# Gates ahead of values in the projection order, a new start and DVE order of the mLSTM chunks, and an output projection begun inside the attention

## The chip, the cores and the metric

The kernel runs on one core of one Trainium2 chip. The metric is the device time of one execution in microseconds. Engines: TensorE (PE, matmuls), ScalarE (ACT), VectorE (DVE), GpSimd (POOL) and SyncE (SP, which issues most DMAs). They run beside each other and meet at semaphores.

## The reference

Two transformer blocks over 1024 tokens of width 1024. The change touches only the mixer of the first:

```python
proj = h @ w_in          # query/key of the mLSTM, v_ml, o_ml, gates, q_at, kv_at
qk_ml = silu(causal_dwconv(qk_ml))
# per chunk and head, with the running state C, n:
sqk = (q @ k.T) * exp(dmat - m_t)
h   = (sqk @ v + w_inter * (q @ C.T)) / max(|den|, exp(-m_t))
h_ml = rms_norm(h, ml_norm_g) * sigmoid(o_ml)
o_at = sliding_window_attention(rope(q_at), rope(k_at), v_at, sinks)
o_at = rms_norm(o_at, attn_norm_g)
y = concatenate([h_ml, o_at]) @ w_out
x = x + g1 * rms_norm(y, post_mix_g)     # g1 and the like: silu(c) @ w_ada
```

A feed-forward block and a whole second block follow; they take the other 1988 us and are not touched.

## The kernel before

Each fp32 product is three fp32r matmuls of 128x128 by 128x512: operands and weights are split into a high and a low part (hhi, hlo; whi, wlo). A weight tile (128 columns, all eight rows of tiles, 512 KB) is loaded by SP, its high part is cut by ACT (`split_hi`, L214) and its low part by DVE (`split_lo`, L219), and it costs PE 48 matmuls, 10.9 us in full (`product`, L294 to L296).

**Product stage.** The input projection has N_IN = 22 tiles: 0 to 5 query, key and value of the attention, 6 to 13 mLSTM query and key with a convolution of three DVE steps (L1154), 14 to 17 mLSTM values, 18 to 21 output gates (sigmoid, spilled to DRAM by POOL). PE's product t waits for `up_free`, that is for the evacuation of product t-2. Beside this DVE adds up the last four adaLN segments, 32 rows of w_ada of 512 KB, each loaded by SP into one of three slots (L960) and added by DVE (L400, L401) at three per tile from tile 8 on (`late_at`). After the product behind the one in which a segment closes, PE waits for its eight rows and reduces it. In DVE's program the rows of tile t stand behind its convolution. The masks are added (L940) and exponentials taken (L946) in tiles 20 and 21.

**Chunks.** Eight chunks of 128 tokens. PE per chunk c: `outputs(c)` (L1396, L1399), `turn_back(c-2)` (L1408), `turn(c+2)` (L1369 to L1371), `update(c+1)` (L1381). ACT copies tokens (L1332, L1333), squares (L1339) and takes the root (L1346, L1348), and in chunks 2 to 5 copies attention keys (L1558). DVE per chunk: copy of the last head (L1442), new state (L1453), denominators (L1463 to L1469), gating of c-2 (L1486), scaling of c-1 (L1476 to L1480), weights of c+2 (L1438). `outputs(c+1)` waits for `scale(c-1)`, whose PSUM bank it writes. Two slots hold the gate tiles that SP loads back (L1280), each behind `c_done`; the gain rows (L1253) stand behind it in the same queue. The first query block of the attention is loaded (L1690) after all of them.

**Attention.** Eight blocks of 128 queries, two units each: scores (PE), maxima (DVE, L1897), exponentials (ACT, L1710), scaling (POOL, L1778), transposes (PE, L1828), split of the probabilities (ACT L1731, DVE L1924), values (PE, L1850 to L1852). Blocks 1 to 6 run in a hardware loop of three trips. Its operands lie in hhi and hlo.

**Output projection.** In the next block (a barrier lies between), `Mix` makes the eight operand tiles: 0 to 3 the mLSTM's, 4 to 7 the attention's after its norm. PE multiplies weight tiles 0 and 1 by operand tiles 0 and 1, then does eight fp32 sum matmuls of 128x512 over the squares (`sum_squares`, L338), then the other operand tiles (L363 to L365); the third product follows.

## Time and profile before

| | |
|---|---|
| median of 3 runs | 2482.6 us (2482.34 to 2487.81) |
| profiled execution, its own time | 2482.53 us |
| its span, first to last instruction | 2480.7 us |
| mean granted TensorE clock | 0.991 |
| PE, DVE, ACT, POOL busy | 96%, 50%, 34%, 14% |

Timelines give each instruction (or run of equal ones, xN) its start and duration. In brackets stands how long the engine was idle before it and what it waited for. Matmuls are pipelined, so their durations overlap and the distance of two starts is what one costs. 0.0 is the first instruction.

### The profile page before, as it was taken

Reading aid. Unit: us, or ns where it says so; the run is one execution under the profiler, and the core shown is the slowest. Engines: PE = TensorE matmul, PEld = TensorE weight load, DVE = VectorE, ACT = ScalarE, POOL = GpSimd, SP = SyncE. Lnnn points to the kernel's source line nnn. Section 1 sums busy time; section 2 is a strip of 40 time slices with the busy share of each in tenths; the row PEclk is TensorE's granted clock in tenths of the full one; section 3 lists DMA queues with packets and bytes.
Section 4 is the critical chain, followed back from the end, with each engine's and each line's share of the span. In section 5 each row is a group of like instructions: output and inputs, shape, how many; then the busy total and the mean of one; then the engine's idle time right before and its main releaser. Section 6 shows DMA issues by size and latency. Waiting matters only on the chain. (4 is left out here: it accounts for less than half of the span.)

```text
span 2480.7 us, 28558 instructions
## 1 busy us (share of the span) xinstructions
PE 2387.0 (96%) x10880; PEld 1927.7 (78%) x10880; DVE 1247.8 (50%) x1492; ACT 833.0 (34%) x1234; POOL 346.5 (14%) x268
## 2 busy tenths in 40 slices
PE   7999978899999999999998989999999999999999
PEld 5788877576888888888876767767888888888887
DVE  6467357437544444444456489963533333333334
ACT  5232267634322222222244368862311111111111
POOL 1120044132000000000032456621000000000000
PEclk9999999999999999999999999999999999999999
DMA  8246532122211111111124220012111111111111
GB/s 325 76 137 210 166 99 74 60 74 89 67 51 43 41 51 51 44 49 51 43 102 141 77 68 26 17 52 68 52 51 51 51 51 41 43 51 51 51 47 72
DMA packets 192733, 183.78 MB, mean 74 GB/s; under 512 B 8505, under 2 KB 170633, under 8 KB 192145
## 3 DMA queue, kind: packets, MB, share of 16 engines
q1 hardware_dynamic: 189984, 175.21, 22.1%
q0 software_dynamic: 2208, 7.37, 0.9%
q8 instruction: 49, 0.80, 0.1%
q14 instruction: 27, 0.22, 0.0%
q10 hardware_dynamic: 465, 0.17, 0.0%
HBM read 154.38 MB, written 28.34 MB: 74 GB/s over the span
## 5 line engine op out<-in xcount | busy, mean ns | idle before, releaser
L294 PE MATMUL ps<-hhi,whi 128*128 128x512 f32 x1696 | 662.8, 391 | 4.5 <-DVE wlo L219 2.0
L296 PE MATMUL ps<-hhi,wlo 128*128 128x512 f32 x1696 | 660.0, 389 | 0.0
L295 PE MATMUL ps<-hlo,whi 128*128 128x512 f32 x1696 | 659.8, 389 | 0.0
L219 DVE TENSOR_TENSOR wlo<-raw,whi 128x1024 fp32r<-128x1024 f32 x178 | 226.4, 1274 | 379.5 <-ACT whi L214 379.4
L294 PEld LDWEIGHTS ps<-hhi,whi 128*128 128x128 f32 x1696 | 318.3, 188 | 72.7 <-DVE wlo L219 2.4
L295 PEld LDWEIGHTS ps<-hlo,whi 128*128 128x128 f32 x1696 | 318.4, 188 | 67.1 <-issue 1.2
L296 PEld LDWEIGHTS ps<-hhi,wlo 128*128 128x128 f32 x1696 | 318.3, 188 | 66.4
L214 ACT ACTIVATE whi<-raw 128x1024 fp32r<-128x1024 f32 x178 | 184.5, 1049 | 387.4 <-PE ps L2420 286.4
L2573 DVE TENSOR_TENSOR arena<-arena,ps 128x1024 f32<-128x1024 f32 x152 | 185.4, 1220 | 128.2 <-PE ps L2420 127.3
L2418 PE MATMUL ps<-hid_hi,whi 128*128 128x512 f32 x608 | 237.6, 391 | 0.0
L2419 PE MATMUL ps<-hid_lo,whi 128*128 128x512 f32 x608 | 236.7, 389 | 0.0
L2420 PE MATMUL ps<-hid_hi,wlo 128*128 128x512 f32 x608 | 236.6, 389 | 0.0
L758 POOL TENSOR_TENSOR cbuf<-cbuf 128x512 f32<-128x512 f32 (+1 forms) x54 | 80.0, 1489 | 890.6 <-ACT cbuf L745 887.6
L2537 DVE SCALAR_TENSOR_TENSOR cbuf<-ps,par,cbuf 128x1023 f32<-128x1023 f32 x44 | 56.4, 1282 | 226.0 <-ACT cbuf L2444 226.0
L1778 POOL TENSOR_TENSOR cbuf<-cbuf,attn_stats 128x1024 f32<-128x1024 f32 x80 | 151.5, 1894 | 95.4 <-DVE attn_stats L1917 95.4
L2418 PEld LDWEIGHTS ps<-hid_hi,whi 128*128 128x128 f32 x608 | 114.1, 188 | 26.8 <-DVE arena L2573 3.3
L2420 PEld LDWEIGHTS ps<-hid_hi,wlo 128*128 128x128 f32 x608 | 114.1, 188 | 23.9
L2419 PEld LDWEIGHTS ps<-hid_lo,whi 128*128 128x128 f32 x608 | 114.1, 188 | 23.5
L2444 ACT ACTIVATE cbuf<-ps,par 128x1024 f32<-128x1024 f32 x44 | 53.0, 1205 | 222.7 <-PE ps L296 220.4
L2550 DVE TENSOR_TENSOR cbuf<-ps,cbuf 128x1024 f32<-128x1024 f32 x22 | 26.9, 1225 | 175.1 <-PE ps L296 156.5
L2458 ACT ACTIVATE hid_hi<-cbuf 128x1024 fp32r<-128x1024 f32 x44 | 46.5, 1057 | 203.1 <-DVEq L2552 110.0
L1828 PE MATMUL ps<-identF,cbuf 128*128 128x128 f32 x640 | 93.0, 287 | 17.2 <-POOL cbuf L1778 14.3
(343 smaller groups left out, 3363.8 us busy)
## 6 DMA issues: line engine op xcount, KB each, us to landing
raw<-in_w_up SPq DMA_DIRECT2D x66, 512.0 KB, 3.6
raw<-in_w_down SPq DMA_DIRECT2D x44, 512.0 KB, 3.4
raw<-in_w_in SPq DMA_DIRECT2D x32, 512.0 KB, 5.1
arena<-in_w_ada SPq DMA_DIRECT2D x32, 512.0 KB, 5.1
raw<-in_w_gate SPq DMA_DIRECT2D x22, 512.0 KB, 3.6
raw<-in_w_out SPq DMA_DIRECT2D x16, 512.0 KB, 3.7
arena<-x_park SPq DMA_DIRECT2D x2, 4096.0 KB, 12.2
x_park<-arena SPq DMA_DIRECT2D x4, 2048.0 KB, 8.8
```

The costliest lines, as they stand in the source:

```text
L214: nc.scalar.activation(whi[:, w.off % RING, :], raw[:, w.off % RAW, :], ACT.Copy).then_inc(hi_done, 1)
L219: nc.vector.tensor_tensor(wlo[:, w.off % RING, :], raw[:, w.off % RAW, :], whi[:, w.off % RING, :].bitcast(F32), ALU.subtract).then_inc(lo ...
L294: nc.tensor.matmul(acc[:, tok], whi[:, s, ws], hhi[:, k, tok], start=(k == 0), stop=False)
L295: nc.tensor.matmul(acc[:, tok], whi[:, s, ws], hlo[:, k, tok], start=False, stop=False)
L296: mm = nc.tensor.matmul(acc[:, tok], wlo[:, s, ws], hhi[:, k, tok], start=False, stop=(k == DK - 1))
L758: nc.gpsimd.tensor_tensor(total, total, cbuf[:, self.slot(r, k), tok], ALU.add).then_inc(self.added[r], 1)
L1778: nc.gpsimd.tensor_tensor(p, p, st[:, sl, 16:16 + q].unsqueeze(2).to_broadcast([P, q, T // q]), ALU.mult).then_inc(S["scaled"], 1)
L1828: mm = nc.tensor.transpose(ps_t[:, (4 * h + k) * P:(4 * h + k + 1) * P], src, identF[:, :])
L2418: nc.tensor.matmul(o, whi[:, s, ws], hidhi[:, p, tok], start=(r == 0), stop=False)
L2419: nc.tensor.matmul(o, whi[:, s, ws], hidlo[:, p, tok], start=False, stop=False)
L2420: mm = nc.tensor.matmul(o, wlo[:, s, ws], hidhi[:, p, tok], start=False, stop=(r == 1))
L2573: nc.vector.tensor_tensor(y[:, fo, :], y[:, fo, :], down[fo % 2][:, :], ALU.add)\
```

## The change

Gates become tiles 14 to 17 and values 18 to 21. The adaLN rows go four to a tile. Masks and exponentials move to tiles 18 to 20, the broadcast rows are loaded earlier, and PE's first turn waits head by head for the last value tiles. Gate tiles get a third slot, the first query block is loaded ahead of the chunk loop, ACT copies the keys in chunks 0 to 3 and DVE subtracts them in chunks 3 and 5; DVE scales c-1 right behind the new state. In the attention the operands move so that hhi 0 to 2 and hlo 0 are free: POOL makes high parts of tiles 0 to 2 in block 0, and squares and adds of the first 512 tokens in blocks 5 to 7; DVE makes the low parts. In the last unit PE does the first half's sum and operand tiles 0 and 1. The attention's loop has two trips and blocks 5 and 6 are unrolled. Behind the barrier the norm goes by halves, with squares added in pairs by POOL before two sum matmuls per half. Left out below: index changes to the third slot, to the tile numbers of gates and values, and the removed body of `Mix`.

```diff
...
                 r = o - T_IN
-                return columns(a["w_in"], w + (20 if r < 2 else 14 if r < 6 else -6), 8 if r < 6 else 0)
+                shift = 20 if r < 2 else 14 if r < 6 else -6 if r < 14 else -2 if r < 18 else -10
+                return columns(a["w_in"], w + shift, 8 if r < 6 else 0)
...
         def kind_of(t):
-            return "qkv" if t < 6 else "conv" if t < 14 else "v" if t < 18 else "o"
+            return "qkv" if t < 6 else "conv" if t < 14 else "o" if t < 18 else "v"
...
-            return range(max(0, 3 * (t - LATE_FROM)), max(0, min(late_rows, 3 * (t - LATE_FROM + 1))))
+            return range(max(0, 4 * (t - LATE_FROM)), max(0, min(late_rows, 4 * (t - LATE_FROM + 1))))
...
+        EXP_FROM = 18
...
                       .then_inc(late_loaded[n % 3], 16)
-                if t == N_IN + 2:
+                if t == N_IN - 1:
...
                     nc.scalar.activation(query_hi_of[n % 2], cbuf[:, (t - 2) % 4, :], ACT.Copy).then_inc(query_hi, 1)
-                if t >= N_IN - 2:
-                    act.wait_ge(g_dve, 13)
-                    for c in range(4 * (t - N_IN + 2), 4 * (t - N_IN + 3)):
+                if t in (EXP_FROM + 1, EXP_FROM + 2):
+                    if t == EXP_FROM + 1:
+                        nc.scalar.preload_act_table_set(LN_EXP)
+                        act.wait_ge(g_dve, 13)
+                    for c in range(4 * (t - EXP_FROM - 1), 4 * (t - EXP_FROM)):
...
                     modulate(ADA_FIRST + seg, down[1][:, seg * DK:(seg + 1) * DK]).then_inc(late_done, 1)
-                if t == N_IN - 2:
-                    for c in range(NB):
+                if t in (EXP_FROM, EXP_FROM + 1):
+                    for c in range(4 * (t - EXP_FROM), 4 * (t - EXP_FROM + 1)):
...
-        def chunk_sp(sp):
+        def chunk_sp(sp, first_query):
...
                 sp.wait_ge(spilled[i], 64)
-            sp.wait_ge(used, N_IN)
-            for b in range(2):
+            multiplied(sp, At(N_IN - 1))
+            for b in range(3):
                 sp.dma_start(gate_tok[b], spill[:, 0:4, tok(b)]).then_inc(gate_in[b], 16)
+            for i in range(2):
+                sp.wait_ge(hi_stored[i], 64)
+            first_query()
...
                     gain_load(sp, c + 2)
-                sp.wait_ge(c_done, c - 1)
-                sp.dma_start(gate_tok[c % 2], spill[:, 0:4, tok(c)]).then_inc(gate_in[c % 2], 16)
-            for i in range(2):
-                sp.wait_ge(hi_stored[i], 64)
+                if c >= 3:
+                    sp.wait_ge(c_done, c - 2)
+                    sp.dma_start(gate_tok[c % 3], spill[:, 0:4, tok(c)]).then_inc(gate_in[c % 3], 16)
...
                 rstd(c)
-                if 2 <= c < 6:
-                    keys.act_key(act, (c - 2) // 2, c % 2)
+                if c < 4:
+                    keys.act_key(act, c // 2, c % 2)
...
                 for h in range(ML_H):
+                    if c == 0:
+                        pe.wait_ge(up_free, N_IN - 1 + h)
...
                     new_state(c)
-                denominators(c)
+                    if c:
+                        scale(c - 1)
+                    denominators(c)
+                else:
+                    denominators(c)
+                    scale(c - 1)
...
                     gated(c - 2)
-                if c:
-                    scale(c - 1)
...
                     weigh(c + 2)
-                else:
-                    keys.dve_keys(dve, c + 2 - NB)
+                if c in (3, 5):
+                    keys.dve_keys(dve, (c - 3) // 2)
...
             kn = T + pad
-            o = 4 * kn
-            khh = lflat[:, 0:2 * kn].rearrange("p (g t) -> p g t", g=2)
-            klo = lflat[:, 2 * kn:o].rearrange("p (g t) -> p g t", g=2)
+            k0 = 0 if full else T
+            o = k0 + 4 * kn
+            khh = lflat[:, k0:k0 + 2 * kn].rearrange("p (g t) -> p g t", g=2)
+            klo = lflat[:, k0 + 2 * kn:o].rearrange("p (g t) -> p g t", g=2)
...
             else:
-                pths, ptls = [[hflat[:, 1024 * (2 * i + j):1024 * (2 * i + j + 1)].rearrange("p (k x) -> p k x", x=ptile)
+                pths, ptls = [[hhi[:, 3 + 2 * i + j, :].rearrange("p (k x) -> p k x", x=ptile)
                                for i in range(2)] for j in range(2)]
-                vband = [hflat[:, 4096 + 512 * i:4096 + 512 * (i + 1)] for i in range(2)]
+                vband = [hhi[:, 7, half(i)] for i in range(2)]
...
                 body(At(0), True)
-                with eng.Fori(0, 3) as i:
+                with eng.Fori(0, 3 if full else 2) as i:
...
                     body(At(2, i, 2), True)
+                if not full:
+                    body(At(5), True)
+                    body(At(6), True)
...
+            def mixing(n, at):
+                return not full and n.i is None and n.off == at
...
                             fetch(n + 1)
-                    lead.sp(sp)
-                    query_blocks(sp, lambda: fetch(At(0)), body)
+                    if full:
+                        lead.sp(sp)
+                        query_blocks(sp, lambda: fetch(first_block), body)
+                    else:
+                        lead.sp(sp, lambda: fetch(first_block))
+                        query_blocks(sp, lambda: None, body)
...
                             u, gr = unit(n, e), group(n, e)
+                            if mixing(n, 7) and e == 1:
+                                mix.act_first_root(act)
...
                             band(At(0))
+                            mix.pool_high(pool, 0)
...
                                 lead.pool_unit(pool, e)
+                            if mixing(n, 0):
+                                mix.pool_high(pool, 1 + e)
+                            if mixing(n, 5) and e == 0:
+                                pool.wait_ge(S["out"], NB)
+                            if mixing(n, 5) or mixing(n, 6):
+                                mix.pool_square(pool, 2 * (n.off - 5) + e)
+                            if mixing(n, 6) and e == 0:
+                                mix.pool_add(pool, 0)
+                            if mixing(n, 7) and e == 0:
+                                mix.pool_add(pool, 1)
...
                                 scores(n, e + 2)
+                            if mixing(n, 7) and e == 1:
+                                pe.wait_ge(S["sink_arg"], 2 * NB)
+                                mix.pe_first_sum(pe)
+                                pe.wait_ge(S["exp"], 2 * NB)
+                                mix.pe_tile(pe, 0)
...
                                     values(gr_before(n, e), ((e - 1) // units) % 2, unit(n, e) + (-1))
+                        if not more and not full:
+                            mix.pe_tile(pe, 1)
...
                             split_probs(n, e)
+                            if mixing(n, 0) and e == 1:
+                                mix.low(dve, 0)
+                            if mixing(n, 7) and e == 0:
+                                mix.low(dve, 1)
+                                mix.low(dve, 2)
...
             def __init__(self):
...
+                self.squared, self.added, self.summed, self.log_done, self.rstd_done = (
+                    sem("mix_" + x) for x in ("squares", "squares_added", "sums", "logs", "rstd"))
...
+                self.op_hi, self.op_lo, self.lows = sem("mix_hi"), sem("mix_lo"), DK + 4
+                self.u0 = n_up[0]
...
+            def square_of(self, h, j):
+                return cbuf[:, (2 if h == 0 else 0) + j // 2, half(j % 2)]
+            def sums(self, h):
+                return down[1][:, half(1)] if h == 0 else down[0][:, half(0)]
+            def root(self, h):
+                return self.square_of(h, 1)
+            def pool_high(self, pool, j):
+                nc.gpsimd.tensor_copy(hhi[:, j, :], self.tile(j)).then_inc(self.op_hi, 1)
+            def pool_square(self, pool, j):
+                q = qa[:, j, half(0)]
+                nc.gpsimd.tensor_tensor(self.square_of(0, j), q, q, ALU.mult).then_inc(self.squared, 1)
+            def pool_add(self, pool, pair, h=0):
+                total = self.square_of(h, 2 * pair)
+                pool.wait_ge(self.squared, 4 * h + 2 * pair + 2)
+                nc.gpsimd.tensor_tensor(total, total, self.square_of(h, 2 * pair + 1), ALU.add).then_inc(self.added, 1)
+            def pool(self, pool):
+                for pair in range(2):
+                    self.pool_add(pool, pair, 1)
+            def pe_sum(self, pe, h):
+                for pair in range(2):
+                    pe.wait_ge(self.added, 2 * h + pair + 1)
+                    mm = nc.tensor.matmul(self.sums(h), onesF[:, :], self.square_of(h, 2 * pair), start=(pair == 0),
+                                          stop=(pair == 1))
+                mm.then_inc(self.summed, 1)
+            def pe_first_sum(self, pe):
+                self.pe_sum(pe, 0)
+            def pe_tile(self, pe, k, halves=(0, 1)):
+                if k == 0:
+                    for t in range(2):
+                        pe.wait_ge(up_free, self.u0 + t + 1)
+                        pe.wait_ge(lo_done, T_OUT + t + 1 + RAW)
+                for t in range(2):
+                    s = (T_OUT + t) % RING
+                    ws = slice(k * P, (k + 1) * P)
+                    for h in halves:
+                        pe.wait_ge(self.op_lo, k + 1 if k < 4 else 4 * h + k + 1)
+                        tok, o = half(h), up[t][:, half(h)]
+                        nc.tensor.matmul(o, whi[:, s, ws], hhi[:, k, tok], start=(k == 0), stop=False)
+                        nc.tensor.matmul(o, whi[:, s, ws], hlo[:, k, tok], start=False, stop=False)
+                        mm = nc.tensor.matmul(o, wlo[:, s, ws], hhi[:, k, tok], start=False, stop=(k == DK - 1))
+                    if k == DK - 1 and halves[-1] == 1:
+                        mm.then_inc(used, 1)
+            def pe_pair(self, pe, w, u0):
+                self.pe_tile(pe, 2)
+                self.pe_tile(pe, 3)
+                self.pe_sum(pe, 1)
+                for h in range(2):
+                    for k in range(4, DK):
+                        self.pe_tile(pe, k, (h,))
+            def act_root(self, act, h):
+                r = self.root(h)
+                act.wait_ge(self.summed, h + 1)
+                nc.scalar.activation(r, self.sums(h), ACT.Ln, bias=eps, scale=1.0 / 512).then_inc(self.log_done, 1)
+                act.wait_ge(self.log_done, h + 1)
+                nc.scalar.activation(r, r, ACT.Exp, scale=-0.5).then_inc(self.rstd_done, 1)
+            def act_first_root(self, act):
+                self.act_root(act, 0)
...
             def act(self, act):
...
+                def hi(h, j):
+                    act.wait_ge(self.product, 4 * h + j - 3)
+                    nc.scalar.activation(hhi[:, j, half(h)], qa[:, j - 4, half(h)], ACT.Copy).then_inc(self.op_hi, 1)
+                nc.scalar.activation(hhi[:, 3, :], self.tile(3), ACT.Copy).then_inc(self.op_hi, 1)
...
+                    nc.scalar.activation(self.square_of(1, j), qa[:, j, half(1)], ACT.Square).then_inc(self.squared, 1)
...
+                    hi(0, j)
+                self.act_root(act, 1)
+                for j in range(4, DK):
+                    hi(1, j)
+                    if j >= 6:
+                        split_hi(act, At(T_OUT + j - 6 + AHEAD))
+            def low(self, dve, j):
+                dve.wait_ge(self.op_hi, j + 1)
+                nc.vector.tensor_tensor(hlo[:, j, :], self.tile(j), hhi[:, j, :].bitcast(F32), ALU.subtract)\
+                  .then_inc(self.op_lo, 1)
...
             def dve(self, dve):
...
+                self.low(dve, 3)
+                for h in range(2):
+                    dve.wait_ge(self.rstd_done, h + 1)
+                    for i in range(5):
+                        if i < 4:
+                            q = qa[:, i, half(h)]
+                            nc.vector.scalar_tensor_tensor(out=q, in0=q, scalar=par_col("attn_norm_g", i),
+                                                           in1=self.root(h), op0=ALU.mult,
+                                                           op1=ALU.mult).then_inc(self.product, 1)
+                        if i >= 1:
+                            j = 3 + i
+                            dve.wait_ge(self.op_hi, 4 * h + j + 1)
+                            nc.vector.tensor_tensor(hlo[:, j, half(h)], qa[:, i - 1, half(h)],
+                                                    hhi[:, j, half(h)].bitcast(F32), ALU.subtract).then_inc(self.op_lo, 1)
...
+        mixing_norm = Mix()
+        attention("attn", False, FirstLead, cbuf[:, 2, :], cbuf[:, 3, :], mixing_norm)
```

## Rows read from the trace of the kernel before

**Rows 1.** Windows: bounds, length; busy PE, PEld, DVE, ACT, POOL; clock, DMA, GB/s.

```profile
318.30:380.60 62.30, 43.73 (x341) 42.03 (x340) 38.08 (x118) 35.58 (x113) 26.84 (x26) 0.92 0.31 90
```

**Rows 2.** Timeline of PE, chunks: start, duration, instruction, count, [idle before, releaser].

```profile
325.98 0.48 PE L1369 MATMUL ps<-identF,arena 128*128 128x128 f32 x1 [5.73 <-ACT chunk_work L1333]
...
330.93 1.06 PE L1396 MATMUL ps<-chunk_work 128*128 128x129 f32 x8
...
341.50 0.46 PE L1396 MATMUL ps<-chunk_work 128*128 128x129 f32 x2 [2.31 <-DVE chunk_work L1480]
...
347.03 0.46 PE L1396 MATMUL ps<-chunk_work 128*128 128x129 f32 x2 [0.41 <-DVE chunk_work L1480]
...
351.10 1.06 PE L1381 MATMUL ps<-chunk_work 128*128 128x129 f32 x8
...
353.56 0.46 PE L1396 MATMUL ps<-chunk_work 128*128 128x129 f32 x2 [1.40 <-DVE chunk_work L1480]
...
371.19 0.46 PE L1396 MATMUL ps<-chunk_work 128*128 128x129 f32 x2 [3.07 <-DVE chunk_work L1480]
...
380.61 0.47 PE L1808 MATMUL ps<-bandR,identR 128*128 128x512 f32 x1 [2.88 <-DMA gateR<-query_parts]
```

**Rows 3.** Timeline of ACT, the beginning of the chunks.

```profile
316.41 4.79 ACT L946 ACTIVATE arena<-arena,gateF 128x128 f32<-128x128 f32 x16
...
323.55 1.28 ACT L1350 ACT_TABLE_LOAD   x1
...
324.84 0.60 ACT L1332 ACTIVATE chunk_work<-ps 128x512 f32<-128x512 f32 x1
```

**Rows 4.** Timeline of DVE, chunk 3.

```profile
349.30 1.12 DVE L1453 SCALAR_TENSOR_TENSOR chunk_work<-chunk_work,gateF,ps 128x129 f32<-128x129 f32 x4
...
353.13 0.28 DVE L1480 TENSOR_SCALAR chunk_work<-chunk_work 128x128 f32<-128x128 f32 x1
```

**Rows 5.** Timeline of PE, end of the attention and first pair of w_out.

```profile
450.79 1.09 PE L1828 MATMUL ps<-identF,cbuf 128*128 128x128 f32 x8 [1.18 <-POOL cbuf L1778]
...
455.33 0.40 PE L1852 MATMUL ps<-hhi 128*64 128x512 f32 x1
...
460.61 0.77 PE L363 MATMUL ps<-hhi,whi 128*128 128x512 f32 x1 [4.88 <-DVE hlo L2057]
...
467.63 7.03 PE L338 MATMUL ps<-cbuf,onesF 128*128 128x512 f32 x16
...
492.48 0.50 PE L294 MATMUL ps<-hhi,whi 128*128 128x512 f32 x1 [0.67 <-ACT arena L2122]
```

**Rows 6.** Timeline of ACT in the same stretch.

```profile
458.14 2.00 ACT L2026 ACTIVATE hhi<-arena 128x1024 fp32r<-128x1024 f32 x2 [1.61 <-PEq L1677]
...
490.49 1.03 ACT L745 ACTIVATE cbuf<-ps 128x1024 f32<-128x1024 f32 x1 [5.29 <-PE ps L365]
```

**Rows 7.** Timelines of DVE, ACT and SP in the product stage.

```profile
185.64 4.05 DVE L401 SCALAR_TENSOR_TENSOR arena<-arena,small 128x1024 f32<-128x1024 f32 x3
...
191.45 1.21 ACT L1052 ACTIVATE cbuf<-ps,par 128x1024 f32<-128x1024 f32 x1 [3.68 <-PE ps L296]
...
232.31 2.38 SPq L960 DMA_DIRECT2D arena<-in_w_ada  x3
...
235.94 1.28 DVE L401 SCALAR_TENSOR_TENSOR arena<-arena,small 128x1024 f32<-128x1024 f32 x1 [0.46 <-DMA arena<-in_w_ada]
```

**Rows 8.** Timelines of POOL and DVE; last, the page's group of weight splits.

```profile
343.68 1.27 POOL L1289 TENSOR_TENSOR lead_work<-arena 128x512 f32<-128x512 f32 x1 [3.12 <-PE ps L1399]
...
440.64 1.90 POOL L1778 TENSOR_TENSOR cbuf<-cbuf,attn_stats 128x1024 f32<-128x1024 f32 x1 [2.11 <-DVE attn_stats L1917]
...
549.28 12.48 POOL L758 TENSOR_TENSOR cbuf<-cbuf 128x512 f32<-128x512 f32 x8
...
553.29 2.32 DVE L219 TENSOR_TENSOR wlo<-raw,whi 128x1024 fp32r<-128x1024 f32 x1
...
L219 DVE TENSOR_TENSOR wlo<-raw,whi 128x1024 fp32r<-128x1024 f32 x178 | 226.4, 1274 | 379.5 <-ACT whi L214 379.4
```

79 lines of the change are left out of this document (19 added, 60 removed).

## The prediction, made before the changed kernel was run

> **What bounds it now.** I read the page first: TensorE is busy for 96% of the span, so time can be won only where it stands idle or does work that can go. The slices of the page show that in few places, and windows cut at the stage bounds say where: in the chunks of the mLSTM (318.3 to 380.6) PE is busy 43.7 of 62.3 us at a granted clock of 0.92 [rows 1], while in w_out's first pair it is busy, but in part with fp32 sums and at half clock. The third reading is PE's timeline across these stages, with what released each wait [rows 2], and then the engine that was late: ACT at the start [rows 3], DVE in the chunks [rows 4], and in the tail PE's own extra work, the block's end and ACT [rows 5, 6]. The product stage ahead of 318.3 has no PE wait at all, so there the change can only lose [rows 7].
>
> All sums are on the clock of the profiled execution (2482.53 us around a span of 2480.7). The median of the runs is 2482.6, so a difference carries over unchanged.
>
> **A. Product stage, late adaLN rows by fours: +2.3.** Moving gates to tiles 14 to 17 reorders loads of equal size and costs nothing: an evacuation is one ACT pass either way. But tiles 8 to 15 now bring four w_ada rows each, not three, and segments close at tiles 9, 11, 13 and 15, where PE waits for all eight rows one product later. In tile 9 the convolution's end lets DVE begin adding at 185.64, and three adds last 4.05, or 1.33 apart [rows 7]. Three slots hold three rows, so SP can ask for the block's fourth row only when the first is added, at 186.97. The nearest landing is that of the row asked for at 232.31 and used at 235.94, 3.63 later [rows 7]. So the fourth is there at 190.6 and added at 191.95. PE would want the segment at about 191.2, just ahead of the evacuation at 191.45 [rows 7]: 0.75 late. Three segments close in convolution tiles, 3 x 0.75 = 2.3; the fourth closes in a gate tile without convolution, and I cost it at nothing. Bounds: 0 if a row lands in 2.8, and +9 if each lands 2.3 later, as may be when several loads share the DMA engines. Queued behind DVE's wait are the split of a weight tile, used two products later, and the next convolution, which has over 5 us of slack; SP's next loads wait behind the row too, with a tile or more in hand. The exponents and exponentials (4.79 per four chunks on ACT [rows 3]) move to tiles 18 to 20, where one tile of 10.9 us holds them, an evacuation and a split: nothing.
>
> **B. The beginning of the chunks: -6.8.** Now PE has turned chunk 0 and then waits 5.73 before it turns chunk 1 at 325.98, because ACT first ends the exponentials begun at 316.41 (4.79), loads a table, does the last sigmoid, loads a table at 323.55, and only then copies chunk 0's tokens at 324.84 [rows 2, 3]. After the change ACT has one copy of the last value tile (about 1.0, ending at 319.6); PE turns heads 0 to 2 beside it and head 3 at 319.7 to 320.1, tokens are copied from 320.35 to 321.4, PE goes on at 321.5. The idle time is then 1.3 instead of 5.73, and after 2.31 us idle at 341.5 later in this stage the clock was still full, so chunk 1's turn takes 1.8 and not 3.5. With the update (0.9) the first outputs begin at 324.1, not 330.93 [rows 2]: -6.8. If the clock falls all the same it is -4.5. The Trainium skill (ScalarE: Activation LUTs, What ACT_TABLE_LOAD costs) puts a switch of tables at 2.66, of which 1.38 is a drain. Here the load at 323.55 is followed by its first activation at 324.84, 1.29 later [rows 3]; no row shows a drain. By the page the two loads would be worth 2.8 more, by the rows they are inside the 6.8; the rows decide.
>
> **C. The chunks' order: -7.3.** DVE did denominators, gating of chunk c-2 and only then the scaling of c-1, which frees the PSUM bank that outputs c+1 want. For outputs 4: the new state is under way at 349.30 and lasts 1.12, scaling ends only at 353.4 (353.13 + 0.28), and PE starts at 353.56 [rows 2, 4]. Right behind the new state (0.15 and 0.56 and 0.28 with their hand-overs, some 0.85) scaling ends at 351.2, so outputs 4 could begin at 351.4. PE's own work from outputs 3 at 347.03 to the end of the update that begins at 351.10 takes 4.96 (351.10 + 0.89) [rows 2]. So PE becomes its own bound at 4.96 per chunk, against 6.5 here and 6.0 on average from outputs 3 to 7 ((371.19 - 347.03) / 4). The new queue on DVE is 4.3 us per chunk, on ACT 4.3 with a key copy (1.05, now in chunks 0 to 3). The two key subtractions (1.2) fall behind the last weighing of chunks 3 and 5, where DVE would wait. Outputs 3 to 7: three times 4.96 and a last 4.5 (no turn to fill in) = 19.4 against 24.2, -4.8. Outputs 0 to 3: 13.2 against 16.1, -2.9. I give back 0.4 for small DVE steps that stand behind Pool now and then. The third gate slot takes SP's wait for c_done off the gain rows behind it in the queue; that only keeps them from being late. Bounds -3 to -8.5.
>
> **D. The chunks' end: -3.2.** From outputs 7 (371.19) to the first scores (380.61) go 9.4 [rows 2]. The scores waited 2.88 for the query DMA, asked for only when all chunk loads had gone; it is now ahead of them. What is late next is the scaling of chunk 7: denominators, squares, root and scaling end 6.2 after outputs 7 start, since the key subtraction and the gating ahead are gone. Bounds -2 to -3.7 (with the clock).
>
> **E. In the attention: +1.4.** Pool gains three copies of 128x1024 in block 0, four squares of 128x512 and one add in blocks 5 and 6, one add in block 7. A 128x512 operation took it 1.27, and scaling 1.89 in a pitch of 4.0 to 4.2 [rows 8], so one square fits behind each scaling (3.16), but not square and add (4.43): +0.3 to +0.6 once. In block 0 the second copy ends some 0.9 after the next scaling is wanted and DVE's subtraction (1.2) has 0.9 to 1.1 of idle time to hide in: +0.8. Nothing else is moved past; the two unrolled blocks replace one loop trip. Bounds 0 and +4.
>
> Rows for a rule that speaks against this: DVE's weight split at 553.29 took 2.32, against a mean of 1.27 for all 178, while Pool ran eight adds from 549.28 on [rows 8]. The Trainium skill (SBUF - State Buffer, SBUF: two separate sides) says that a VectorE operation with two SBUF inputs and a GpSimd operation that reads SBUF exclude each other for the whole instruction. The row agrees; the sum above takes the slots as free, and a rival below takes them as not.
>
> **F. Output projection: -10.2.** Now the last product of the values starts at 455.33, ACT begins the next block at 458.14, PE at 460.61 after 4.88 idle, first at half clock; eight fp32 sums take 7.03; the third product starts at 492.48 [rows 5, 6]. After: two sums (2 x 0.81) and 12 products (12 x 0.2275 = 2.73) go ahead of the last transposes, 12 more ahead of the last values. Of these 7.1 us 1.18 fall into idle time ahead of the last transposes (450.79) and the rest of the difference into the wait ahead of the last values: these start their last product 4.6 later, at 459.95, and the next block begins at 462.75 [rows 5]. Left are 6 tiles x 12 x 0.2275 = 16.4 and two sums = 18.0: end at 480.8 against 491.65. ACT and DVE have each operand ahead of PE: first half-tile product at 467, wanted at 470; second half at 473.9, wanted at 475.5. The evacuation begins at 480.3 instead of 490.49, product three at 482.3: -10.2. The x load (4 MB) is asked for 7.6 earlier, product three comes 10.2 earlier; the weight tile behind it is wanted over 10 us later, so no loss. If PE's 2.4 idle at the block's end halves its clock, it is -8.8. Bounds -7.5 and -11.
>
> **Sum.** 2.3 - 6.8 - 7.3 - 3.2 + 1.4 - 10.2 = -23.8; 2482.5 - 23.8 = 2458.7. The 1988 us behind shift as a whole.
>
> **Rivals.** (1) The chunk pitch doesn't fall: the root of c-1 (squares 1.6 and root 0.6 behind the token copies) takes the place of the order. For it: ACT does 4.3 per 4.96; against: it ends some 0.6 ahead of need. Then C loses 5.5: 2464. (2) Rows land late in A: 5.5 instead of 3.6 makes the three stalls 2.6 each: 2464 to 2466. For it: loads bunch. (3) Pool and DVE shut each other out: eleven new Pool operations, each costing 1.05 as at 553.29, are 11.6 in place of 1.4: 2469. Against: most stand where DVE waits for ACT. The rule cited under E is this case's. (4) The change doesn't do what it says in F: PE's idle time there is only moved, since the projection's early part delays the last values and the operands behind them: F is -4, 2465. (5) Slower: the fourth row again. It stalls PE by its landing less 2.9, three times; the change as a whole loses more than 7.4 only if that eats 31 us, from a landing of 13.3 on. The landing shown is 3.63 [rows 7]. 2490.
>
> **Chances.** Forecast 0.62, own range 2453 to 2463; (1) 0.13, (2) 0.09, (3) 0.06, (4) 0.05, (5) 0.02; two or more of them together 0.03, near no change. Range 2452 to 2470. A measurement here can tell 0.3%, 7.4 us, from no change: faster 0.94, within 0.03, slower 0.03.
>
> **What would show it.** A: PE waits for a DVE add of 0.5 to 1 us, three times ahead of the adaLN reductions. B: first outputs 5.8 us behind the last product. C: outputs 4.9 to 5.2 apart. D: no DMA wait ahead of the scores. E: attention pitch still 4.0 to 4.2. F: the third product starts 19.5 us after ACT's first step of that block. It would be wrong if outputs stay 6 apart, if PE waits for an operand in the half tiles, or if the clock falls at the seams.

## The result, and the profile after

The changed kernel takes 2473.1 us (median of 6 runs, 2471.57 to 2476.78), the kernel before 2485.2 beside it (6 runs, 2482.34 to 2487.81): ratio 0.995, 95% interval 0.994 to 0.9961. It is faster, by half of what I forecast: 12.1 us in place of 23.8. The two profiled executions are 2482.53 and 2475.31, only 7.2 apart, since the one sits low among its kernel's runs and the other high; the table is in their clock, and adds up to the 7.4 between their spans. A negative number is time won.

| Stage | before | after | forecast | measured |
|---|---|---|---|---|
| start to the first convolution tap | 143.02 | 142.37 | 0 | -0.65 |
| tap to the end of the last product (A) | 175.30 | 187.98 | +2.3 | +12.68 |
| to outputs 0 (B) | 12.61 | 5.83 | -6.8 | -6.78 |
| outputs 0 to 7 (C) | 40.26 | 35.80 | -7.3 | -4.46 |
| outputs 7 to first scores (D) | 9.42 | 8.34 | -3.2 | -1.08 |
| first scores to third product (E, F) | 111.87 | 101.85 | -8.8 | -10.02 |
| third product to the end | 1988.22 | 1991.13 | 0 | +2.91 |
| span | 2480.7 | 2473.3 | -23.8 | -7.4 |

One stage holds most of the miss. The product stage, where PE had no wait at all before, now loses 12.7 us. The timeline of PE in the changed kernel (start, duration, instruction; in brackets the idle time before it and who ended it) has three waits there, all at the fp32 sums that close an adaLN segment:

```profile
194.55 3.57 PE L345 MATMUL ps<-onesF,arena 128*128 128x1 f32 x16 [3.79 <-DVE arena L402]
...
223.62 1.92 PE L345 MATMUL ps<-onesF,arena 128*128 128x1 f32 x16 [1.07 <-DVE mod L406]
...
248.82 1.92 PE L345 MATMUL ps<-onesF,arena 128*128 128x1 f32 x16 [1.41 <-DVE mod L406]
```

The first is 3.79 us, where I had said 0.75, and the sums behind it take 3.57 in place of 1.84 to 1.92: half clock (the granted clock is 0.50 from 194 to 203, that is 1.2 and not 2.4 GHz). The windows of ten microseconds (busy time of PE, PEld, DVE, ACT, POOL; then the granted clock) show how long it lasts:

```profile
190.00:200.00 10.00, 6.21 (x25) 5.37 (x24) 7.32 (x7) 2.15 (x2) 0.00 (x0) 0.66 0.74 262
200.00:210.00 10.00, 10.00 (x39) 8.05 (x38) 6.58 (x6) 2.12 (x2) 0.00 (x0) 0.83 0.74 258
210.00:220.00 10.00, 10.00 (x46) 8.29 (x45) 6.77 (x6) 2.27 (x2) 0.00 (x0) 1.00 0.09 20
...
250.00:260.00 10.00, 10.00 (x41) 8.20 (x41) 5.65 (x5) 2.75 (x3) 0.58 (x1) 0.83 0.86 292
```

Who was late is in the other timelines. ACT's, in the same stretch:

```profile
181.87 1.06 ACT L214 ACTIVATE whi<-raw 128x1024 fp32r<-128x1024 f32 x1 [6.58 <-DMA raw<-in_w_in]
182.84 1.19 ACT L1056 ACTIVATE cbuf<-ps,par 128x1024 f32<-128x1024 f32 x1
188.06 1.06 ACT L1059 ACTIVATE arena<-cbuf 128x1024 f32<-128x1024 f32 x1 [4.02 <-DVE cbuf L1158]
194.70 1.06 ACT L214 ACTIVATE whi<-raw 128x1024 fp32r<-128x1024 f32 x1 [5.58 <-DMA raw<-in_w_in]
195.66 1.19 ACT L1056 ACTIVATE cbuf<-ps,par 128x1024 f32<-128x1024 f32 x1
```

ACT waits 5 to 7 us for a weight tile, eight times in this stage. The tap (L1056), which begins a tile's convolution and so frees its PSUM, stands behind that split in ACT's order: it starts at 182.84, not when its product ends. SyncE's queue and DVE say why the tile is late:

```profile
176.27 13.29 SPq L962 DMA_DIRECT2D arena<-in_w_ada  x4
189.67 0.38 SPq L208 DMA_DIRECT2D raw<-in_w_in  x1
```

```profile
178.92 1.28 DVE L402 SCALAR_TENSOR_TENSOR arena<-arena,small 128x1024 f32<-128x1024 f32 x1 [1.28 <-DMA arena<-in_w_ada]
182.97 1.23 DVE L219 TENSOR_TENSOR wlo<-raw,whi 128x1024 fp32r<-128x1024 f32 x1 [2.76 <-ACT whi L214]
184.11 3.91 DVE L1158 SCALAR_TENSOR_TENSOR cbuf<-ps,par,cbuf 128x1023 f32<-128x1023 f32 x3
187.94 4.05 DVE L402 SCALAR_TENSOR_TENSOR arena<-arena,small 128x1024 f32<-128x1024 f32 x3
193.21 1.29 DVE L402 SCALAR_TENSOR_TENSOR arena<-arena,small 128x1024 f32<-128x1024 f32 x1 [1.21 <-DMA arena<-in_w_ada]
```

The four row loads from 176.27 on take up 13.29 us of the queue. The last of them is the fourth row of the product: its slot is free when DVE has added the product's first row, at 187.94 + 1.33 = 189.3, and there the queue goes on. It lands in about 3.9 (added at 193.21), near the 3.63 of [rows 7]. But the load of the next weight tile goes out only at 189.67, behind it, and ACT has it at 194.70, where it wanted it at 189.1. In the kernel before the load in the same place goes out 8 us ahead of its split, which waits for nothing; but two tiles later a split does wait, if only 0.24 (SyncE's queue and ACT):

```profile
178.74 1.14 SPq L208 DMA_DIRECT2D raw<-in_w_in  x1
...
186.73 1.04 ACT L214 ACTIVATE whi<-raw 128x1024 fp32r<-128x1024 f32 x1
...
208.83 1.06 ACT L214 ACTIVATE whi<-raw 128x1024 fp32r<-128x1024 f32 x1 [0.24 <-DMA raw<-in_w_in]
```

### The profile page after: what moved, and what is told of

The parts are those of the page before. It is cut to its first block and busy times, and to the rows that moved or that the text cites. A ratio compares the mean times of both kernels' runs of the same rounds, so it can differ in the third digit from the quotient of the medians.

```text
span 2473.3 us, 28496 instructions
## 1 busy us (share of the span) xinstructions
PE 2388.8 (97%) x10872; PEld 1930.1 (78%) x10872; DVE 1252.9 (51%) x1500; ACT 824.5 (33%) x1233; POOL 359.3 (15%) x279
## 5 line engine op out<-in xcount | busy, mean ns | idle before, releaser
L1862 PE MATMUL ps<-identF,cbuf 128*128 128x128 f32 x640 | 92.3, 287 | 17.0 <-POOL cbuf L1802 12.8
```

The lines of the kernel that those rows point to most:

```text
L1862: mm = nc.tensor.transpose(ps_t[:, (4 * h + k) * P:(4 * h + k + 1) * P], src, identF[:, :])
```

## Experiments

Four kernels first, to tell the queue from the landing, and a side question on the chunks. (The fourth of them, with its companion, was made last, after all the others.) Kernels were run in batches, each beside the kernel before; where two batches are compared, the ratio to it says more than the time. In all of them the stage is measured from the first tap to the end of the last product.

**Only the rows by fours, on the kernel before.**

```diff
-            return range(max(0, 3 * (t - LATE_FROM)), max(0, min(late_rows, 3 * (t - LATE_FROM + 1))))
+            return range(max(0, 4 * (t - LATE_FROM)), max(0, min(late_rows, 4 * (t - LATE_FROM + 1))))
```

> The kernel before with one edit of the change: adaLN rows by fours (4 per product from product 8 on, in 3 slots) in place of threes. Theory Q (SyncE's queue): the fourth row of a product waits in SyncE's queue for the add of the first row of the same product, and the load of the next weight tile stands behind it, so ACT gets its weight tile 5 to 7 us late and evacuates late. The last product then ends 10 to 13 us later than the 318.3 of the kernel before, and the time is before +10 to +13. Theory L (the prediction's step A: only the landing of the fourth row counts, 0.75 us at each of three segment ends): before +2.3.

Measured: 2500.9 against 2488.14, ratio 1.0048 (1.0031 to 1.0065), 12.8 us slower. The stage takes 189.17 (+13.9), with PE waits of 3.16, 1.00 and 0.98, as theory Q had it. The loss belongs to this one edit; without the rest the kernel would have become slower than before.

**The changed kernel with rows by threes.**

```diff
-            return range(max(0, 4 * (t - LATE_FROM)), ...
+            return range(max(0, 3 * (t - LATE_FROM)), ...
...
-                if t == N_IN - 1:
+                if t == N_IN:
                     sp.wait_ge(rows_stored, 16)
...
-        EXP_FROM = 18
+        EXP_FROM = 19
...
-                if t in (EXP_FROM, EXP_FROM + 1):
-                    for c in range(4 * (t - EXP_FROM), 4 * (t - EXP_FROM + 1)):
+                if t == EXP_FROM + 1:
+                    for c in range(NB):
                         exponents(dve, c)
```

> The changed kernel with its rows by threes again (products 8 to 18); the exponents and exponentials are one and two products later (20; 20 and 21), and SyncE asks for the exponent rows behind the load of tile 22. All else as in the changed kernel. Theory Q: the last product ends at 317 to 319, not at 330.4, everything behind it keeps its lengths, and the time is that of the changed kernel less 11 to 12.5, some 2461 to 2462. Theory L: less 2.3, 2471. A third theory (the 12 us come from values behind gates, or from the earlier exponentials): no gain at all.

Measured: 2462.13, ratio 0.9898 (0.9881 to 0.9914). The stage is 175.30 again, to the hundredth, without a wait, so the gates ahead of the values cost nothing there. The exponentials are in tiles 20 and 21 again in this kernel, as in the kernel before, so it says nothing on them; the next one, which has them early, does. It pays elsewhere: outputs 0 begin 8.44 behind the last product and not 5.83. PE waits 0.81 in the first turn of the beginning and 1.18 ahead of the second here (the changed kernel has the 1.18 alone), and then runs slow: step B's -4.5 for a clock that falls (12.61 to 8.44 is -4.2).

**A fourth slot.** Rows stay by fours.

```diff
-        late_row = [ar(48 + 4 * i, D) for i in range(3)]
+        late_row = [ar(48 + 4 * i, D) for i in range(3)] + [ar(32, D)]
...
-                    if n >= 3:
-                        sp.wait_ge(late_added, n - 2)
...
+                    if n == 3:
+                        sp.wait_ge(rows_stored, 16)
+                        sp.wait_ge(gains_stored, 16)
+                        sp.wait_ge(g_pe, 1)
+                    if n >= 4:
+                        sp.wait_ge(late_added, n - 3)
...
```

> The changed kernel with rows by fours, and a fourth slot for them (in the space of the values, which is written from product 18 on): the fourth row of a product waits only for the product before. Number, size and order of the loads stay. Theory Q: SyncE is no longer held inside a product, the 5 to 7 us waits of ACT for weight tiles go, the last product ends at 317 to 320, time as with threes to within 1.5 us (2461 to 2463). Theory of the landings (four rows and a weight tile share the DMA engines, so they come late whatever the queue does): last product still at 325 or later, 2468 or more. A PE wait at the ends of the segments of 0 to 1 us each may stay in both.

Measured: 2460.61, ratio 0.9894 (0.9878 to 0.9911). The stage takes 175.52 and PE has no wait in it. The same 32 rows and the same weight tiles move in the same order; only what SyncE waits for and the place of one row in four are different. So it isn't the amount of traffic, and the exponentials in tiles 19 and 20 cost 0.2 at most. ACT still waits for one weight tile, 7.08 ahead of its split at 247.62, and PE doesn't notice it.

**One weight tile later in the queue.** Three slots, rows by fours, one number:

```diff
-                for n in late_at(t - 2):
+                for n in late_at(t - 3):
```

> The changed kernel (three slots, rows by fours) with one number changed: SyncE asks for the rows of a product one weight tile later in its queue (rows of product t-3 behind the load of tile t, not of product t-2). The fourth row still waits for the first add of its product, but the load behind it is one that ACT wants a whole product later. Theory Q: ACT's waits of 5 to 7 us for weight tiles go, and what is left of the 12.7 us that the product stage lost is the fourth row's own landing ahead of the adaLN reductions, the prediction's 2.3 (0 to 3.5): last product's end 177.5 after the first tap (175.3 in the kernel before, 188.0 in the changed kernel), time 2461 to 2464. If the landing of four rows, not the queue, were the cause, the stage stays at 184 or more and the time at 2469 or more.

And beside it the changed kernel unaltered:

> The changed kernel unaltered, on the same chip as the one above. All theories: 2473, ratio to before 0.995; the product stage takes 188 from the first tap to the last product's end and the stage behind the third product 1988 to 1991.6, by the number of norm sums that meet half clock.

Measured: swap 2468.44, ratio 0.993 (0.9916 to 0.9943); the unaltered changed kernel beside it 2472.12, ratio 0.9944 (0.993 to 0.9957). The intervals overlap a little, but the slowest run of swap (2470.6) is faster than the fastest of the other (2471.24). This is between my two expectations, and it splits the loss. The groups of instructions of ACT from 175 to 290 (count, busy time, mean ns, idle time before them) in the changed kernel, and then in this one:

```profile
L214 ACT ACTIVATE whi<-raw 128x1024 fp32r<-128x1024 f32 x10 | 10.6, 1057 | 45.4 <-DMA raw<-in_w_in 45.4
```

```profile
L214 ACT ACTIVATE whi<-raw 128x1024 fp32r<-128x1024 f32 x10 | 10.5, 1047 | 0.0
```

45.4 us of waiting for weight tiles are gone, and yet the stage takes 183.56: 8.3 more than before. What is left is the fourth row's own landing and what follows it, in PE's timeline of this kernel:

```profile
192.99 1.95 PE L345 MATMUL ps<-onesF,arena 128*128 128x1 f32 x16 [0.84 <-DVE arena L402]
194.79 0.48 PE L295 MATMUL ps<-hhi,whi 128*128 128x512 f32 x1
...
219.44 1.92 PE L345 MATMUL ps<-onesF,arena 128*128 128x1 f32 x16 [0.98 <-DVE mod L406]
```

and in its windows:

```profile
190.00:200.00 10.00, 9.16 (x42) 7.38 (x41) 8.62 (x8) 3.21 (x3) 0.00 (x0) 0.83 0.69 243
...
240.00:250.00 10.00, 9.05 (x43) 7.39 (x42) 7.20 (x8) 2.92 (x3) 0.58 (x1) 0.86 0.99 360
```

The waits are 0.84, 0.98 and 0.95: 2.8 in all, and the 2.3 that step A had worked out, nearly. But behind two of the three PE runs eight products at a pitch of 0.43 and not 0.227. For all kernels I add up the waits, and the time lost to slow clock (each product's pitch over 0.3, less 0.227, without the 0.5 that the same count gives at full clock, and what the sums take over 1.9):

| Kernel | stage | waits of PE | slow clock |
|---|---|---|---|
| before, threes | 175.30 | 0 | 0 |
| fourth_slot | 175.52 | 0 | 0 |
| swap | 183.56 | 2.77 | 4.7 |
| changed | 187.98 | 6.27 | 5.7 |
| changed, again | 189.48 | 5.52 | 7.6 |
| keys_late | 189.21 | 5.29 | 7.7 |
| fours_alone | 189.17 | 5.14 | 7.6 |

Waits and clock together are all but 0.7 to 1.1 of each loss, and in four of the five kernels the clock is the larger part. In the last three and in swap 1.6 to 2.9 of it stands at 147 to 156, behind 3 us of small fp32 products of 4x4 and 4x8 and with no wait near; the other kernels, the changed one in its first trace among them, have the same products there and no slow clock. All four have rows by fours in three slots. Whether that plays a part stays open.

**Key subtractions in chunks 6 and 7.**

```diff
-                if c in (3, 5):
-                    keys.dve_keys(dve, (c - 3) // 2)
+                if c in (6, 7):
+                    keys.dve_keys(dve, c - 6)
```

> The changed kernel with DVE's two key subtractions (1.22 us each) in chunks 6 and 7, where they were before, not in 3 and 5. Theory K (the subtraction of chunk 5 makes the scaling late that outputs 7 wait for): the wait of 3.60 us ahead of outputs 7 falls to 2.0 to 2.6, PE's clock stays full there, outputs 3 to 7 take 20.5 and not 21.9, outputs 7 to the first scores 6.2 to 7.2 and not 8.3; in all -2 to -3.5, 2470. Theory P (Pool's operations that run beside DVE's small SBUF operations make the scaling late): the wait stays within 0.5 of 3.6, and the subtraction in chunk 7 is hidden behind the root; within 1 us of the changed kernel.

Measured: 2473.68, ratio 0.9938 (0.9922 to 0.9955), where the changed kernel has 0.995 (0.994 to 0.9961) and, in its second batch, 0.9944: no gain that can be told. The wait ahead of outputs 7 falls from 3.60 to 2.46 and outputs 3 to 7 from 21.94 to 20.08, as theory K said, and the way to the first scores is 8.69 and not 8.34. But the unaltered kernel's second trace has 3.21 and 20.77, and swap, with the subtractions in 3 and 5, has 2.67: one trace can't carry a difference of this size. Whether the place matters isn't shown.

The second four are on the fourth-slot kernel, which no longer has the disturbance of step A.

**Chunks 3 and 6.**

```diff
-                if c in (3, 5):
-                    keys.dve_keys(dve, (c - 3) // 2)
+                if c in (3, 6):
+                    keys.dve_keys(dve, (c - 3) // 3)
```

> The fourth-slot kernel with DVE's two key subtractions in chunks 3 and 6 (not 3 and 5, nor 6 and 7). Theory K: in chunk 6 the subtraction stands behind everything that outputs 7 wait for, and not ahead of the scaling of chunk 7, so outputs 3 to 7 take about 20.1 as in keys_late (against 21.15), and outputs 7 to the first scores 6.2 as in fourth_slot (8.69 in keys_late): 1 us under fourth_slot, ratio to before 0.989. Theory P (Pool's beat sets this stage): no change to 0.5 us.

Measured: 2459.77, ratio 0.9893 (0.9877 to 0.991), the same as fourth_slot's 0.9894 to what can be told. Outputs 0 to 7 take 34.16 and not 35.01, then 8.32 and not 6.20: its outputs 7 ran at half clock. The 0.8 us are less than the 1.2 by which outputs 0 to 7 differ in two traces of the unaltered changed kernel (35.80 and 34.63), so whether the place is worth anything stays open.

**DVE's order in the chunks undone.**

```diff
                 if c + 1 < NB:
                     new_state(c)
-                    if c:
-                        scale(c - 1)
-                    denominators(c)
-                else:
-                    denominators(c)
-                    scale(c - 1)
+                denominators(c)
                 if c >= 2:
                     gated(c - 2)
+                if c:
+                    scale(c - 1)
```

> The fourth-slot kernel with DVE's order in the chunks as before: denominators of c, gating of c-2, then the scaling of c-1; nothing else. If the order is what shortens the chunks (the prediction's step C, 7.3 us, of which 4.8 from outputs 3 to 7): outputs 3 to 7 take 24 to 25 and not 21.15, outputs 0 to 3 16, waits for the scaling of 0.4 to 1.5 us ahead of each outputs again, time 4 to 6 us over fourth_slot, some 2466. If the pitch fell for another reason (exponentials, gates and query out of the way): within 1.5 us of fourth_slot.

Measured: 2467.08, ratio 0.9929 (0.9905 to 0.9952). Outputs 0 to 3 take 17.12 (13.86 in fourth_slot), 3 to 7 25.33 (21.15), and PE waits 1.16 to 2.16 for the scaling ahead of every outputs from 2 to 6. The order is worth 7.4 in the trace and 6.5 in the medians (8.7 by the ratios). It is the whole of step C: with the old order outputs 0 to 7 take 42.45, not even the 40.26 of the kernel before, so the chunks' other edits shorten nothing there by themselves.

**Pool's gating multiplication made short.** The output lacks most of the norm's gains.

```diff
-                nc.gpsimd.tensor_tensor(gate_tok[c % 3], gate_tok[c % 3],
-                                        par_col("ml_norm_g", 0, 4).unsqueeze(2).to_broadcast([P, ML_H, P]),
+                nc.gpsimd.tensor_tensor(gate_tok[c % 3][:, :, 0:4], gate_tok[c % 3][:, :, 0:4],
+                                        par_col("ml_norm_g", 0, 4).unsqueeze(2).to_broadcast([P, ML_H, 4]),
                                         ALU.mult).then_inc(c_gain, 1)
```

> The fourth-slot kernel, but Pool multiplies by the norm's gains only 4 of the 128 positions of each head of a chunk's gates, so eight operations of 1.04 us become short ones; the rest of that multiplication is left out. Theory P (DVE's smallest operations with both operands in SBUF, L1469 to L1486 of the changed kernel, last 0.8 to 1.0 instead of 0.15 to 0.28 where they meet a Pool operation): four to nine such long ones become two to four, outputs 0 to 7 take 1.5 to 2.5 less than 35.0, ratio to before 0.0008 lower. If PE's own work and the root's chain set the pitch: 0.5 us or less, though the DVE operations get shorter all the same.

Measured: outputs 0 to 7 take 32.74 where fourth_slot has 35.01; 2456.31, ratio 0.9878 (0.9862 to 0.9895), some 4 us under fourth_slot's, with intervals that overlap. The timelines of DVE and then of Pool in fourth_slot show the cause, chunk 4:

```profile
347.90 1.00 DVE L1486 TENSOR_TENSOR chunk_work<-chunk_work 128x4 f32<-128x4 f32 x1
348.94 0.56 DVE L1488 TENSOR_TENSOR chunk_work<-ps,chunk_work 128x384 f32<-128x384 f32 x1
349.41 0.28 DVE L1490 TENSOR_SCALAR chunk_work<-chunk_work 128x128 f32<-128x128 f32 x1
349.60 0.15 DVE L1473 TENSOR_TENSOR chunk_work<-ps,gateF 128x3 f32<-128x3 f32 x1
349.67 0.94 DVE L1473 TENSOR_TENSOR chunk_work<-chunk_work,gateF 128x1 f32<-128x1 f32 x1
```

```profile
347.84 1.04 POOL L1311 TENSOR_TENSOR chunk_work<-chunk_work,par 128x512 f32<-128x512 f32 x1
349.46 1.13 POOL L1305 TENSOR_TENSOR chunk_work<-chunk_work,gateF 128x516 f32<-128x516 f32 x1 [0.57 <-ACT chunk_work L1343]
```

and in the kernel with the short multiplication, the same instruction of DVE:

```profile
346.07 0.17 DVE L1486 TENSOR_TENSOR chunk_work<-chunk_work 128x4 f32<-128x4 f32 x1
```

An operation on four columns takes 1.00, and ends at 348.90, when Pool's ends (347.84 + 1.04). The one on three columns that reads PSUM takes 0.15 at 349.60, with Pool at work beside it; the next, on one column with both operands in SBUF, takes 0.94 and ends at 350.61, again with Pool's (350.59). Of 19 such operations between outputs 0 and 7 (one or four columns, both operands in SBUF), seven are long in fourth_slot (5.1 us too much in all), eight in the changed kernel (5.9) and two in the kernel with the short multiplication (1.0). The unaltered changed kernel's second trace has five (3.4), and there outputs 0 to 7 take 34.63 in place of 35.80. The scaling of the fourth head (L1490, 128x128, one tensor from SBUF) is long too at times: 0.78 and 0.99 in place of 0.28 in fourth_slot, never with the short multiplication. This is the rule of the Trainium skill (SBUF — State Buffer, SBUF: two separate sides) that I had cited for the attention: whichever of the two starts first has the shared port for its whole instruction. The trace agrees: an operation of a single column with both operands in SBUF ends with Pool's, to 0.02 us.

**The output projection undone.** Attention loop, places and projection as before; chunks as changed.

```diff
-                            if mixing(n, 7) and e == 1:
-                                pe.wait_ge(S["sink_arg"], 2 * NB)
-                                mix.pe_first_sum(pe)
-                                pe.wait_ge(S["exp"], 2 * NB)
-                                mix.pe_tile(pe, 0)
...
-        attention("attn", False, FirstLead, cbuf[:, 2, :], cbuf[:, 3, :], mixing_norm)
+        attention("attn", False, FirstLead, cbuf[:, 2, :], cbuf[:, 3, :])
```

> The fourth-slot kernel with the output projection as before: no part of it inside the attention, norm over the whole row, ACT makes the operands; attention loop and places in SBUF as before, chunk part unchanged. The prediction's step F with E (10.2 less 1.4): first scores to third product 110.5 to 112 and not 100.5, time 9 to 10.5 over fourth_slot, 2470 to 2471. Rival: step F alone but the cost inside the attention nothing, +11.5; rival: Pool's and DVE's new work costs more than 3 us in the attention and F is worth 12 or more, which shows in a shorter stretch from the first scores to the last values.

Measured: 2472.21, ratio 0.9942 (0.9925 to 0.9958) against 0.9894: 11.9 us, more than the 9 to 10.5 expected and next to the rival's 11.5. Windows cut at the last scores, in the changed kernel and in this one:

```profile
380.32:442.82 62.50, 57.53 (x335) 46.53 (x336) 45.19 (x101) 49.83 (x176) 36.49 (x28) 0.92 0.21 60
442.82:482.17 39.35, 35.18 (x160) 25.75 (x158) 26.49 (x39) 24.84 (x55) 10.68 (x8) 1.00 0.08 28
```

```profile
368.88:432.76 63.88, 58.88 (x336) 47.71 (x336) 43.91 (x100) 49.98 (x176) 29.51 (x21) 0.90 0.20 58
432.76:484.72 51.96, 41.69 (x168) 28.75 (x166) 24.15 (x32) 28.42 (x52) 5.31 (x4) 0.93 0.11 41
```

The tail, from the last scores to the third product, is 39.4 in every kernel that has step F (39.34 to 39.39 in nine traces) and 52.0 here; in the kernel before it is 50.5. The attention ahead of it takes 61.1 to 62.6 in the nine traces with Pool's new operations; without them it is 63.9 here, at a clock of 0.90, and 61.3 and 62.6 in the kernel before and fours_alone, at 0.94 and 0.92: the cost of step E is below what the clock makes of this stretch. So of the 15.3 by which the way from the first scores to the third product is longer here than in fourth_slot, 12.6 are the tail.

## Why the prediction was half right

**A failed, and it is most of the miss.** The arithmetic on the row held: the landing (about 3.9 against 3.63), and waits of 0.84 to 0.98 against 0.75 in the kernel where nothing else is late. Two things were missing. The first is the sentence that cost SyncE's queue at nothing: "SP's next loads wait behind the row too, with a tile or more in hand". The fourth row goes out in the middle of its own product, and whatever stands behind it in the queue goes out then as well. In hand were not a tile or more but the 8 us between 178.74 and 186.73, less the load's own landing: 6.5 in the median in this stage of the kernel before, up to 8.5 (5.0 in the changed kernel). That is 1 or 2 us, and twice it was nothing: the splits at 208.83 and 241.19 wait 0.24 and 3.35 for their tiles in the kernel before already. I had not read those rows. ACT then took the tap late, so DVE began adding late, and a wait of 0.8 became 3.8. The fourth slot and the shift in the queue, which remove this and leave the traffic, settle it.

The second is the clock. I priced a wait of PE at its length; here ten of the fifteen waits in the table's kernels, 0.84 to 3.8 long and all ahead of fp32 sums, were followed by 8 to 12 of the 128x512 products at half clock, which, with the sums where they were slow too, cost another 1.5 to 4.2 each time. The prediction's last sign of being wrong, that the clock falls at the seams, came true.

By the medians the hold in the queue is worth 3.7 (swap against the changed kernel beside it), and the landing with the slow clock some 8 to 9 (swap against fourth_slot, 2468.44 and 2460.61 in two batches; 8.9 by the ratios); of the 8.3 in swap's trace 2.8 are the waits, 3.1 the clock behind two of them, 1.6 the slow clock near 150 that no wait explains, and 0.8 stays unassigned.

The rival of late landings (2) named the right place and the wrong cause. The slower rival (5) had the fourth row, but by its landing alone; its price is also mis-summed, since a loss of 7.4 needs 33.5 in step A against the 26.1 won elsewhere, not 31. The 12.7 measured are under 40% of that, and what the other steps won covered them.

**B was right**: 5.83 behind the last product, 5.8 forecast, the same to 0.01 in nine traces.

**C's mechanism was right, its size too large** by 2.8: 35.80 against 33.0, and 34.63 in the second trace of the same kernel (the order is worth 7.4, in old_order; but outputs 0 to 7 stay at 35.0 even with step A mended). From outputs 1 on they stand 4.85 to 5.98 apart, where 4.9 to 5.2 was said. I gave back 0.4 "for small DVE steps that stand behind Pool now and then". It is 2.3, by pool_quiet, where outputs 0 to 3 take 13.26 and 3 to 7 take 19.48: the 13.2 and 19.4 of the sum before that 0.4 was given back. Rival (3) had this mechanism, in the attention; it acts in the chunks, where DVE is close to being the bound and its shortest instructions are the exposed ones.

**D** was worked out for a full clock: 6.2, and fourth_slot has 6.20. But that is one trace of ten; the others with this end of the chunks have 7.25 to 8.69. The changed kernel has 8.34, since its outputs 7, behind a wait of 3.60, run at half clock. The length of the wait doesn't decide it: fourth_slot waited 2.71 and kept its clock, combo waited 2.45 and lost it. D's bound of -2 was meant for the clock and was missed, with -1.08. Outputs 7 in the changed kernel:

```profile
371.98 0.77 PE L1403 MATMUL ps<-chunk_work 128*128 128x129 f32 x2 [3.60 <-DVE chunk_work L1486]
```

No DMA wait is left ahead of the scores, as said.

**E and F.** -10.0 against -8.8. ACT begins the block at 462.45 and the third product starts at 482.17, 19.7 later (19.5 forecast); the tail as a whole gave 11.2, and the attention ahead of it took 1.2 longer at a lower clock (0.92 against 0.94). E's +1.4 can be neither confirmed nor excluded.

**Behind the third product** I had nothing, and 2.9 went. PE's norm sums behind that product, in the kernel before and then in the changed one:

```profile
558.20 1.12 PE L763 MATMUL ps<-cbuf,onesF 128*128 128x512 f32 x2 [2.45 <-POOL cbuf L758]
...
588.06 1.13 PE L763 MATMUL ps<-cbuf,onesF 128*128 128x512 f32 x2 [1.33 <-POOL cbuf L758]
```

```profile
547.89 1.91 PE L764 MATMUL ps<-cbuf,onesF 128*128 128x512 f32 x2 [2.45 <-POOL cbuf L759]
...
578.70 2.00 PE L764 MATMUL ps<-cbuf,onesF 128*128 128x512 f32 x2 [2.13 <-POOL cbuf L759]
```

Same instructions and the same wait at the first, but half clock. Over twelve traces the stretch from the third product to the end is 1988.1 to 1989.4 where neither of the two is slow, 1989.5 to 1991.1 with one, 1990.8 to 1991.6 with both. It isn't tied to an edit: the unaltered changed kernel had both slow in one trace and neither in the next (1988.5). This may be part of why its profiled run is high among its runs; it is no term of the change.

**The sum without A** was -26.1. With step A mended the kernels measure -26.0 (threes) and -27.5 (fourth_slot) against the runs beside them. That this is so near is in part luck: their traces are only 22.0 and 23.0 shorter than the trace of the kernel before (spans of 2458.7 and 2457.7 against 2480.7), with less than forecast in C and, in threes, in B and D, and more in E and F; the kernel before ran 5.6 slower beside them than in its profiled execution. Both of these, and combo at 2459.8, are 11 to 13 us faster than the changed kernel.

## What to carry to other kernels

Before one more load is put into a queue, ask on what it waits, and then what stands behind it in that queue, and by when that is wanted counted from the new time of issue, not from the old one; one more slot, or one place later in the queue, takes the hold away. Price a new wait of TensorE in a dense stretch at its length and, as a likely case (ten of fifteen here), at 1.5 to 4 us of half clock behind it. Where DVE runs near the bound beside Pool, look at its shortest instructions with both operands in SBUF: each can last as long as the Pool operation that it meets. And before one stage of one trace is compared with another kernel's, look how far two traces of the same kernel lie apart: 1.2 us in 35 here.

## What the runs showed of the hardware

- A DMA issue of SyncE that waited for a semaphore held those behind it: four row loads took up 13.29 us of the queue, and the weight load behind them left 0.1 after.
- Half clock came behind waits of PE of 0.84, 0.93 and 3.79 us, and didn't behind others of 0.98 and 1.07 in the same stage; fp32 sums or small fp32 products were what PE did last before the slow 128x512 products there.
- The same PE instructions behind the same wait of 2.5 us ran at full clock in one execution of the changed kernel and at half in another (1.12 and 1.91 us for two fp32 sum products).
- An ACT table load took 1.28, and the activation behind it started 0.01 after its end.
- An operation of DVE on one column, both operands in SBUF, took 0.94 in place of 0.15, up to the end of Pool's; with PSUM as a source it took 0.15 at the same time.
